# Dense slices of a hybrid recurrent trunk: six matmuls of 272 columns become five of 288, 512 and 256

## The reference

```
layer 0: u = RMSNorm(h) @ ab_w_in          # gated DeltaNet, 8 heads || GLA, 4 heads
         y = [o_dn * silu(z), o_gla * silu(z)] @ ab_w_out
layer 1: u = RMSNorm(h) @ cd_w_in          # SSD, 16 heads || RG-LRU, 1024 channels
         y = [y_ssd, y_lru] @ cd_w_out
each:    h = h + y
         h = h + sigmoid(RMSNorm(h) @ ple_w_gate) * (p @ ple_w_proj)
out:     RMSNorm(h), and the new states of every branch
```

## Time and profile before

| | |
|---|---|
| median of three runs | 2451.63 us (2447.52 to 2455.24) |
| profiled execution, first to last instruction | 2447.1 us |
| TensorE matmul busy | 2384.2 us, 97% |
| VectorE busy | 1280.8 us, 52% |
| ScalarE busy | 958.4 us, 39% |
| mean granted clock of TensorE | 0.993 |

### The profile page before, as it was taken

How to read it: one execution, slowest core, us unless ns; L and a number is a source line. 1 busy time by engine, 2 the same in 40 slices (tenths; PEclk the granted TensorE clock), 3 DMA queues, 4 the chain that set the end, 5 groups by cost and what they waited for, 6 DMA issues and landing times.

```text
span 2447.1 us, 50327 instructions
## 1 busy us (share of the span) xinstructions
PE 2384.2 (97%) x21567; PEld 2273.9 (93%) x21567; DVE 1280.8 (52%) x2387; ACT 958.4 (39%) x1547; POOL 373.5 (15%) x558
## 2 busy tenths in 40 slices
PE   7999999999999999999999999999999999999996
PEld 7998999988999999899999999988899999999996
DVE  6655656565654564622444465566656663243432
ACT  5523444323444344432332353443355553243332
POOL 3101101111101101111111212122212211111111
PEclk9999999999999999999999999999999999999998
DMA  9433333333344454552233343233323354223232
GB/s 232 115 103 107 116 98 116 108 90 106 108 121 117 136 152 122 194 161 87 87 97 109 110 114 92 70 89 87 86 80 103 95 190 127 87 83 96 79 88 76
DMA packets 375535, 271.16 MB, mean 111 GB/s; under 512 B 24419, under 2 KB 346733, under 8 KB 374800
## 3 DMA queue, kind: packets, MB, share of 16 engines
q1 hardware_dynamic: 341424, 172.53, 26.0%
q0 software_dynamic: 22080, 72.77, 9.3%
q10 hardware_dynamic: 11808, 22.63, 2.6%
HBM read 220.24 MB, written 48.37 MB: 110 GB/s over the span
## 4 chain that ended last, share of the span: by engine, by line
PE 86%; DVE 6%; ACT 5%; issue 2%; DMA 1%; POOL 0%; ACTq 0%; DVEq 0%; POOLq 0%
PE psd L582 71%; PE psw L605 2%; PE psw L604 2%; PE psw L632 1%; PE psw L682 1%; DVE arena L1967 1%; PE psw L660 1%; PE psw L668 1%; ACT w_hi L1136 1%; DVE w_lo L1683 1%; PE psw L674 0%; PE psw L646 0%; PE psw L654 0%; PE psw L971 0%; PE psw L1066 0%
## 5 line engine op out<-in xcount | busy, mean ns | idle before, releaser
L582 PE MATMUL psd<-xh,w_hi 128*128 128x272 f32 x5056 | 1098.3, 298 | 8.9 <-DVE w_lo L1683 5.3
L582 PE MATMUL psd<-xl,w_hi 128*128 128x272 f32 x5056 | 1048.4, 289 | 2.9 <-DVE xl L1745 2.1
L582 PE MATMUL psd<-xh,w_lo 128*128 128x272 f32 x5056 | 1045.2, 288 | 0.0
L582 PEld LDWEIGHTS psd<-xh,w_hi 128*128 128x128 f32 x5056 | 795.0, 189 | 60.0 <-issue 40.5
L582 PEld LDWEIGHTS psd<-xh,w_lo 128*128 128x128 f32 x5056 | 796.4, 189 | 0.0
L582 PEld LDWEIGHTS psd<-xl,w_hi 128*128 128x128 f32 x5056 | 792.2, 189 | 4.2 <-DVE xl L1745 3.1
L1683 DVE TENSOR_TENSOR w_lo<-w_raw,w_hi 128x512 fp32r<-128x512 f32 x632 | 433.7, 706 | 380.5 <-ACT w_hi L1136 379.4
L1136 ACT CAST w_hi<-w_raw 128x512 fp32r<-128x512 f32 x632 | 376.7, 616 | 573.2 <-PE psd L582 499.3
L2590 POOL TENSOR_TENSOR states<-states,extra 128x544 f32<-128x544 f32 x59 | 86.7, 1469 | 514.4 <-ACT extra L1191 514.3
L2377 DVE TENSOR_TENSOR extra<-psd,rstd 128x544 f32<-128x544 f32 x32 | 23.2, 724 | 156.0 <-PE psd L582 138.9
L2350 DVE TENSOR_TENSOR arena<-arena,psd 128x544 f32<-128x544 f32 x32 | 23.1, 721 | 136.7 <-PE psd L582 129.9
(11 more groups left out here) (514 smaller groups left out, 2376.9 us busy)
## 6 DMA issues: line engine op xcount, KB each, us to landing
w_raw<-in_ab_w_in_dram SPq DMA_DIRECT2D x224, 256.0 KB, 3.0
w_raw<-in_cd_w_in_dram SPq DMA_DIRECT2D x148, 256.0 KB, 3.0
w_raw<-in_ple_w_gate_dram SPq DMA_DIRECT2D x128, 256.0 KB, 3.1
w_raw<-in_ab_w_out_dram SPq DMA_DIRECT2D x64, 256.0 KB, 2.8
w_raw<-in_cd_w_out_dram SPq DMA_DIRECT2D x64, 256.0 KB, 2.8
uT_scratch<-mix ACTq DMA_DIRECT2D x53, 272.0 KB, 2.2
hT_scratch<-arena POOLq DMA_DIRECT2D x8, 1088.0 KB, 6.4
arena<-hT_scratch POOLq DMA_DIRECT2D x8, 1088.0 KB, 9.5
```

Source lines behind the costliest of these rows:

```text
L582: mm = pe.matmul(out[:, D0 + HALF * half:D0 + HALF * (half + 1)], w[:, r, k % QH, :], x[:, k, HALF * half:HALF * (half + 1)], start=(k == ...
```

## The change

The slice has five matmuls. The tokens are cut at 288 (`NA`) and the last 256 (`NBK`). The first 288 tokens get three matmuls of 288 columns as before, into columns 224 to 512 (`own`). For the last 256 tokens `w_hi` meets the high part and the remainder in one matmul of 512 columns, and the two results land side by side in the second bank (`both`); `w_lo` adds its 256 to the left half. For that `xh` and `xl` lie piece by piece next to each other in one tensor `xhl`. The sum of the last 256 tokens is so left in two halves, and VectorE adds them: in evictions and gates by `join`, a copy of the right half to `low` and an add into the left half in PSUM; in the output projections by a second add of 256 columns to the residual.

```
--- before.py
+++ after.py
@@ -28,9 +28,9 @@
 SSD_XBC = SSD_W + 2 * SSD_G * SSD_N
 LRU_W = 1024
 TAPS = 4
-HALF = T // 2
-D0 = SEQ - HALF
 CUT = SEQ // 2
+NA, NBK = T - CUT, CUT
+D0 = SEQ - NA
 WT = slice(SEQ - CUT, SEQ - CUT + T)
 
 
@@ -224,7 +224,8 @@
 
         psd = [ctx.enter_context(nc.psum_tensor(f"psd{i}", [P, 1024], F32)) for i in range(2)]
         psw = [ctx.enter_context(nc.psum_tensor(f"psw{i}", [P, 1024], F32)) for i in range(2)]
-        xh, xl = sb("xh", [P, KT, T], F32R), sb("xl", [P, KT, T], F32R)
+        xhl = sb("xhl", [P, KT, 2, T], F32R)
+        xh, xl = xhl[:, :, 0, :], xhl[:, :, 1, :]
         arena = sb("arena", [P, KT * T])
         KH = KT // 2
         QH, NW = KT // 4, 6
@@ -257,6 +258,7 @@
         rowR, onehot = sb("rowR", [P, T], F32R), sb("onehot", [P, 2, SSD_H], F32R)
         rstd = sb("rstd", [P, T])
         wa2 = sb("wa2", [P, GLA_KW])
+        low = sb("low", [P, NBK])
 
         C32 = c32[:, 0:6 * 32].rearrange("p (l j) -> p l j", l=6)
         mine2, mine4 = c32[:, 6 * 32:6 * 32 + 2], c32[0:64, 6 * 32 + 2:6 * 32 + 6]
@@ -574,15 +576,16 @@
                     pe.wait_ge(S["x_hi"], KT * ph + k + 1)
                 if k % QH == 0:
                     pe.wait_ge(S["lo_ready"], q + 1)
-                out = psd[d % 2]
-                for i, (w, x) in enumerate(((w_hi, xh), (w_lo, xh), (w_hi, xl))):
-                    if head and i == 2:
-                        pe.wait_ge(S["x_ready"], KT * ph + k + 1)
-                    for half in range(2):
-                        mm = pe.matmul(out[:, D0 + HALF * half:D0 + HALF * (half + 1)], w[:, r, k % QH, :],
-                                       x[:, k, HALF * half:HALF * (half + 1)],
-                                       start=(k == 0 and i == 0), stop=(k == KT - 1 and i == 2))
-                mm.then_inc(S["slice_done"], 1)
+                hi, lo = w_hi[:, r, k % QH, :], w_lo[:, r, k % QH, :]
+                own, both = psd[d % 2][:, D0:SEQ], psd[d % 2][:, SEQ:2 * SEQ]
+                pe.matmul(own, hi, xhl[:, k, 0, 0:NA], start=k == 0, stop=False)
+                pe.matmul(own, lo, xhl[:, k, 0, 0:NA], start=False, stop=False)
+                if head:
+                    pe.wait_ge(S["x_ready"], KT * ph + k + 1)
+                pe.matmul(own, hi, xhl[:, k, 1, 0:NA], start=False, stop=k == KT - 1)
+                pe.matmul(both.rearrange("p (i t) -> p i t", i=2), hi, xhl[:, k, :, NA:T], start=k == 0, stop=False)
+                pe.matmul(both[:, 0:NBK], lo, xhl[:, k, 0, NA:T], start=False, stop=k == KT - 1)\
+                    .then_inc(S["slice_done"], 1)
 
             def fill(to):
                 while at[0] < to:
@@ -1683,12 +1686,19 @@
                 dve.tensor_tensor(w_lo[:, q % NW], w_raw[:, q % NW], w_hi[:, q % NW].bitcast(F32),
                                   ALU.subtract).then_inc(S["lo_ready"], 1)
 
+            def join(d):
+
+                late = psd[d % 2][:, SEQ:2 * SEQ]
+                dve.wait_ge(S["slice_done"], tile_end(d))
+                link(dve.tensor_copy(low[:, :], late[:, NBK:2 * NBK]))
+                link(dve.tensor_tensor(late[:, 0:NBK], late[:, 0:NBK], low[:, :], ALU.add))
+
             def evacuate(d):
 
                 evac[0] = d + 1
                 if TILES[d][3] not in ("ab", "cd"):
                     return
-                dve.wait_ge(S["slice_done"], tile_end(d))
+                join(d)
                 dst = rowlr[:, :]
                 if d in DIRECT:
                     dst = raws[:, T * DIRECT[d]:T * DIRECT[d] + T]
@@ -2347,7 +2357,8 @@
                     dve.wait_ge(S["slice_done"], tile_end(d))
                     if c % 4 == 0:
                         dve.wait_ge(S[f"h_loaded{c // 4}"], 16 * (layer + 1))
-                    dve.tensor_tensor(hT(c), hT(c), psd[d % 2][:, D0:D0 + T], ALU.add)\
+                    link(dve.tensor_tensor(hT(c), hT(c), psd[d % 2][:, D0:D0 + T], ALU.add))
+                    dve.tensor_tensor(hT(c)[:, NA:T], hT(c)[:, NA:T], psd[d % 2][:, SEQ + NBK:SEQ + 2 * NBK], ALU.add)\
                        .then_inc(S[f"dense_read{d % 2}"], 1)
                 lo_part(2 + 3 * layer, KT - 1)
                 fill(first_slice(f"gate{layer}"))
@@ -2366,7 +2377,7 @@
                         fill(SL * (d + 1))
                     else:
                         last_tile(3)
-                    dve.wait_ge(S["slice_done"], SL * (d + 1))
+                    join(d)
                     if c == 0:
                         dve.wait_ge(S["nrm_rstd"], 2 * layer + 2)
                     else:
```

## The result

The changed kernel takes 2477.17 us (median of four runs, 2475.56 to 2482.73) against 2451.16 before in the same round; the ratio is 1.0111, 95% interval 1.0095 to 1.0128. The forecast was 2450 and no change. The profiled execution went from 2447.1 to 2476.6 us.

A forecast was written before the change was run, and what follows sets the result against it. The prediction took TensorE's dense matmul slices as the bound. Its terms, -30.3 + 19 + 1.7 + 3.5 + 4.5 = -1.6 us on the profiled 2447.1, led to 2450 us, no change (chance 0.40, range 2444 to 2459).

The forecast's parts named there:

- the first term: Dense slices on TensorE: one matmul of six fewer saves 12 ns in each of 2528 slices, 30.3 us.
- I cost at nothing: Dense slices: the 512's two runs and three matmuls in a row into one bank, put at no cost.
- The 19 us for layer 0: Layer 0's recurrence: some 26 of 57 evictions, delayed by the join, reach TensorE and cost 19 us.
- The 1.7 for layer 1's recurrence: Layer 1's recurrence: three evictions delayed by the join reach TensorE, 1.7 us.
- The 3.5 for the ends: Starts and ends of output and gate stages: TensorE waits for the added VectorE work, 3.5 us together (1 to 5).
- all 0.92 us: Layer 0's recurrence at 366.99 us: no room behind the eviction's link, so the join's whole 0.92 us reach TensorE.
- rival C: Dense slices: one matmul less saves nothing or little, only the costs stay, +24 us, 2476 us; chance 0.12.
- B: Layer 0's recurrence is set by VectorE; half of 94 evictions delay a link by 0.75 us; 2465 us, chance 0.17.
- What of the gain is lost: TensorE comes earlier to products and loads it already waits for, so 4.5 us of the gain are lost.
- In the gate stage it is busy 16.7 us of 61: VectorE's load in the gate stage, where TensorE was said never to wait.
- the word against the change: Skill page's isolated gap, N/2.4 + 2.5 ns: a matmul saved gives 2.5 ns, 6.3 us in all; 0.04 of C's chance.

The follow-up runs named there:

- the join alone: The kernel before, six matmuls of 272 kept, with a linked copy and add of 240 PSUM columns put into its evictions and gate tiles: 2474.48 us, ratio 1.009.
- by turns without join: The changed kernel with its five matmuls reordered so the two banks take turns, and without the join's copy and add: 2439.29 us, ratio 0.9946 to before.
- the cut at 288: The kernel before with its six matmuls cut at 288 and 256 tokens instead of 272 and 272: 2437.24 us, ratio 0.9943.
- the one run: The changed kernel with its 512-column matmul reading 512 columns in one run, high parts only: 2470.54 us in a single execution.
- the order by turns: The changed kernel, join kept, with its five matmuls reordered so that the two banks take turns: 2466.7 us, ratio to before 1.0058.

## Why the prediction was wrong

**The step that failed** is the first term: "3 x 132 + 225.3 + 118.7 = 740 ns against 751 to 752. Saved: 12 ns x 2528 = 30.3 us." As built the slice measured 752.4 ns over all stages against 752.1, so nothing was saved and some 0.8 us were lost; the changed kernel without join is at 0.9996 of before. The 12 ns that a matmul carries beside its columns were read at 256 to 288 columns and carried to 512. There they are 17 to 22.5 ns, and 22.5 in the changed kernel (235.8 less 213.3). The slope of the earlier trace rows, 0.41 ns a column, is borne out by all such products of that trace (118.2 and 131.4 ns); it doesn't hold beyond 288, where the step from 288 to 408 and from 408 to 512 is 0.45. Six pairs read to 10 ns could not have told the two apart, which differ by 1.4 ns over those 32 columns.

The second part of the failure is what the text put down with "I cost at nothing". The order of the five matmuls is worth 6.6 ns a slice in out0 and 17 us over all stages, more than half of the gain that is missing; the two runs are worth 2 to 3 ns a slice. The text had named both, with "up to all of it", and gave that case 0.12.

**The stalls were sized well.** The 19 us for layer 0, from rows of the kind of the earlier trace rows, measured 18.5: that is what the join alone added to the stage ab. The 1.7 for layer 1's recurrence measured 1.7 (549.2 to 550.9). The 3.5 for the ends: the output and gate stages after, with the last one's end, grew by 5.4 us. Of that 1.2 us are the pace of the slices and up to 1.7 the fall of the clock at 2245 us (both estimates), so 2.5 or a little more are left. In the join alone, which has no second residual add, they grew by 1.1. The link after the eviction of the earlier trace rows was said to pay "all 0.92 us", and the row has 0.92. In all, rival C, the sum without the gain, was 2476, and 2477.17 was measured. That it is so near is in part luck, since C has no term for the clock. The sign given for B, a layer 0 longer by 25 us, nearly appeared (23.6 us in ab) without B's stalls of 35.

**What of the gain is lost** (4.5 us) had nothing to be lost from in the changed kernel. Where there was a gain, the term holds: 16 us of slice time by turns without join, 11.5 of them arrive; 17 us of the cut at 288, 13.6 arrive. So 3.5 to 5 us are lost by the medians (5 to 7 by the profiled executions).

**The sentence on the gate stage.** "In the gate stage it is busy 16.7 us of 61" is read from out0. In gate0 of the kernel before, VectorE is busy 30.4 of 61 us (1250 to 1311 us), still with no idle TensorE, so the argument stands.

**What was not foreseen**: falls of the granted clock in the middle of layer 0. Two kernels with the join and no fall at 532 us, the join alone and the one run, have 1006.9 and 1006.6 us in ab, with one fall of 3.4 us near 732 us. This execution has 1012.0 and 13.6 us of falls there; the 10.2 us more at half clock are 5.1 us by estimate, the whole difference. The falls follow idle spots of TensorE (1.01 us just before 532, some 2 us just before 732), but this execution idled 1.36 us at 513 and 2.01 us at 736 with no fall behind either, so what decides is open.

**On the word against the change.** The trace had 125 ns at 272 columns; the Trainium skill, "TensorE: Matmul & The Clock Gate", section "Back-to-back issue gap", gives N/2.4 + 2.5 ns as the isolated gap and about 131 ns a matmul as the sustained spacing at N = 512. No run here shows either at 512: it is 232 ns in a stream of nothing but 512s at the granted clock 1.00, each with its weight load. By the formula a matmul fewer saves 2.5 ns a slice; as built it saved nothing (752.4 against 752.1), so for the sum the formula was a better guide than my 12 ns.

**What stays open**: what makes a column cost more than 1/2.4 ns. It is not the values of the weights (zero weights), hardly VectorE's work beside it (the means of before are 125.35 ns while VectorE is busy and 125.20 while it is not), and not the number of matmuls alone. Whether it is the reading of operands, the write to PSUM or the weight load that runs beside it was not tried. Nor is it settled why 288 and 256 from column 224 on are cheaper than 256 and 288 from column 256 on, or why the same five matmuls run at 734 ns a slice in one tile of a gate and at 747 in the next.

## What to carry to other kernels

A fixed cost read as a difference between lengths that lie close together must not be carried to a length twice as long: measure that length first, with the banks as they will be used. Instructions moved from the bounding engine to an idle one are not free when that engine's queue holds links of a dependence chain; count the places where such a link stands right behind, since each pays all that its room doesn't cover, however idle the engine is on average. Try the order of the matmuls (here by turns into two PSUM banks, 10.5 us) and the cut of the tokens itself: here each was worth more than the matmul that was saved. Read a pace in more than one stage before it is multiplied by all slices.

## What the runs showed of the hardware

- In out0, three float32r matmuls of 288 columns in a row into one bank stand 132 to 134 ns apart, in the order by turns with another bank 130 to 132.
- In the gate stages the order by turns runs at 734 to 736 ns a slice in some tiles and at 747 in others, mostly every second one, with the same instructions at the granted clock 1.00, and at the same tiles in two kernels.
- In out0, cuts of the same 544 columns differ by up to 1.4% in pace: 288 + 256 has 743.3 ns a slice, 256 + 288 748.3, 272 + 272 751.7, 264 + 280 753.4.
- A stream of 408-column matmuls has 185.0 ns between starts, of 512 columns 232, each with a weight load of its own.
- Zero weights change nothing in the pace: 125.28 ns between starts of 272 columns in both.
- A wait of 1.01 us for VectorE in the recurrence was followed, 0.9 us later, by 10 us at the 1.2 GHz level in one execution; the same wait of 0.98 to 1.02 us in three other kernels was not.
